# A two-layer transformer trunk on one core: the residual update that closes a feed-forward split moves into the next split's first block

## What is computed

```
h = rms_norm(x) * (1.0 + sc2) + sh2
x = x + g2 * swiglu(h, ffn_w_in[layer], ffn_w_out[layer])
# swiglu: gate, up = split(h @ w_in, 2);  (silu(gate) * up) @ w_out
```

## Time and profile before

| what | value |
| --- | --- |
| median of three runs | 2400.76 us |
| lowest and highest run | 2396.38, 2400.95 us |
| span of the profiled execution (its own time) | 2402.0 us |
| TensorE (PE) busy | 2210.0 us, 92% |
| VectorE (DVE) busy | 1744.0 us, 73% |
| ScalarE (ACT) busy | 955.6 us, 40% |
| mean granted TensorE clock | 0.982 of full speed |
| mean DMA rate | 247 GB/s |

### The profile page before, as it was taken

The page is one execution under the profiler, slowest core; times in us unless marked ns, Lnnn a source line. Parts: engine busy times, 40 slices in busy tenths (PEclk is TensorE's granted clock), DMA queues, the critical chain, the costliest instruction groups (busy, mean ns, idle before and its releaser), DMA issues.

```text
span 2402.0 us, 27802 instructions
## 1 busy us (share of the span) xinstructions
PE 2210.0 (92%) x10348; PEld 1841.0 (77%) x10348; DVE 1744.0 (73%) x2089; ACT 955.6 (40%) x1236; POOL 10.1 (0%) x23
## 2 busy tenths in 40 slices
PE   0199999989999999999998999898999999999997
PEld 0178888778888788887886788787888788887886
DVE  6898889898779877898777856498775545554454
ACT  1054444435443344433444344244443344433443
POOL 0000000000000000000000000000000000000000
PEclk9999999999999999999999999899999999999999
DMA  8876776786768877788766632285774455554533
GB/s 334 348 302 271 286 278 245 296 333 250 277 264 330 342 281 287 267 357 314 286 244 250 236 122 99 97 330 220 281 280 174 177 178 190 192 193 175 189 150 151
DMA packets 82438, 593.12 MB, mean 247 GB/s; under 512 B 9409, under 2 KB 9441, under 8 KB 10785
## 3 DMA queue, kind: packets, MB, share of 16 engines
q1 hardware_dynamic: 81056, 587.25, 63.8%
q0 software_dynamic: 1280, 4.51, 0.7%
HBM read 589.62 MB, written 2.10 MB: 246 GB/s over the span
## 4 chain that ended last, share of the span: by engine, by line
PE 43%; issue 36%; DVE 13%; DMA 4%; DVEq 2%; ACT 2%; SPq 0%; POOL 0%; ACTq 0%; POOLq 0%
PE ps L1164 12%; PE ps L1166 12%; PE ps L1165 12%; DVE acc L699 6%; DMA ada_raw<-in_ada 4%; DVE w_lo L677 3%; PE ps L1153 2%; DVE work L970 1%; DVE x L973 1%; DVEq L971 1%; PE ps L1231 1%; PE ps L1236 1%; PE ps L1234 1%; PE ps L1250 0%; PE ps L1248 0%
## 5 line engine op out<-in xcount | busy, mean ns | idle before, releaser
L431 ACT ACTIVATE w_hi<-raw 128x1024 fp32r<-128x1024 f32 x728 | 767.9, 1061 | 1087.8 <-PE ps L1166 989.2
L677 DVE TENSOR_TENSOR w_lo<-raw,w_hi 128x1024 fp32r<-128x1024 f32 x728 | 887.9, 1222 | 427.5 <-ACT w_hi L431 424.4
L1164 PE MATMUL ps<-w_hi,xT_hi 128*128 128x512 f32 x1952 | 773.8, 396 | 31.3 <-DVE w_lo L677 22.5
L1166 PE MATMUL ps<-w_hi,xT_lo 128*128 128x512 f32 x1952 | 765.4, 392 | 0.0
L1165 PE MATMUL ps<-w_lo,xT_hi 128*128 128x512 f32 x1952 | 764.8, 392 | 0.0
L699 DVE SCALAR_TENSOR_TENSOR acc<-ada_raw,cond,acc 128x512 f32<-128x512 f32 (+1 forms) x656 | 485.8, 747 | 19.6 <-DMA ada_raw<-in_ada 12.4
L1164 PEld LDWEIGHTS ps<-w_hi,xT_hi 128*128 128x128 f32 x1952 | 369.7, 189 | 110.4 <-issue 31.9
L1166 PEld LDWEIGHTS ps<-w_hi,xT_lo 128*128 128x128 f32 x1952 | 369.3, 189 | 78.5
L1165 PEld LDWEIGHTS ps<-w_lo,xT_hi 128*128 128x128 f32 x1952 | 369.8, 189 | 74.7
L1164 PE MATMUL ps<-w_hi,hT_hi 128*128 128x512 f32 x960 | 377.3, 393 | 5.0 <-DVE w_lo L677 2.9
L1166 PE MATMUL ps<-w_hi,hT_lo 128*128 128x512 f32 x960 | 374.3, 390 | 0.0
(11 more groups left out here) (145 smaller groups left out, 931.9 us busy)
## 6 DMA issues: line engine op xcount, KB each, us to landing
ada_raw<-in_ada SPq DMA_DIRECT2D x176, 1024.0 KB, 6.6
raw<-in_ffn_in SPq DMA_DIRECT2D x176, 1024.0 KB, 4.8
raw<-in_ffn_out SPq DMA_DIRECT2D x88, 1024.0 KB, 6.3
raw<-in_ab_in SPq DMA_DIRECT2D x48, 1024.0 KB, 7.2
raw<-in_swa_in SPq DMA_DIRECT2D x20, 1024.0 KB, 5.4
raw<-in_ada SPq DMA_DIRECT2D x16, 1024.0 KB, 10.6
raw<-in_ab_out SPq DMA_DIRECT2D x16, 1024.0 KB, 7.0
raw<-in_swa_out SPq DMA_DIRECT2D x16, 1024.0 KB, 7.2
```

The costliest lines, as they stand in the source:

```text
L431: nc.scalar.activation(w_hi[:, p % PAIRS, :, :], raw[:, t % RAW, 2 * (p % 2):2 * (p % 2) + 2, :], ACT.Copy).then_inc(hi_ready, 1)
L677: tt(w_lo[:, p % PAIRS, :, :], raw[:, (p // 2) % RAW, 2 * (p % 2):2 * (p % 2) + 2, :], w_hi[:, p % PAIRS, :, :].bitcast(F32), ALU.subtract ...
L1164: mm(out, hi[:, kt, tok], w_hi[:, q % PAIRS, k, :], start=(kt == 0), stop=False)
L1166: last = mm(out, lo[:, kt, tok], w_hi[:, q % PAIRS, k, :], start=False, stop=(kt == 2 * ph.pairs - 1))
```

## The change

VectorE no longer issues the update of output block 3 behind the output stage of splits 0 and 1. It issues it in the first iteration of the next split's input stage, behind the `lo` of pair 3 (and ahead of that pair's ada step). The semaphore value that it waits for is the same count, written from the new stage's side. No other engine's code is touched.

```
@@ -1024,6 +1024,8 @@
                                     gated(fin, h0, 2 * i + b - 1, 1 - b)
                                 if p == 5 and not (first and b == 0):
                                     hidden_lo(h0, 2 * i + b - 1, 1 - b)
+                                if first and s and n == 3:
+                                    update(NB - 1, 1, USED_CREDIT + 2 * fin.quad0)
                                 if first and summed_in and n in (8, 15):
                                     columns(summed_in, n // 15)
                                 ada_behind(fin, i, n)
@@ -1051,8 +1053,6 @@
                     repeat(dve, 1, fin.n, body)
                     out_body(0, True)
                     repeat(dve, 1, fout.n, out_body)
-                    if s < 2:
-                        update(NB - 1, 1, used(NB - 1))
                     h0 += 2 * fin.n
```

## The result

| | before | changed |
| --- | --- | --- |
| median of the timed runs | 2398.82 us | 2374.51 us |
| lowest and highest | 2396.38, 2400.95 | 2372.14, 2375.92 |
| span of the profiled execution | 2402.0 us | 2370.2 us |
| TensorE's waits for a `lo` | 25.4 us in 13 | 9.0 us in 7 |

The ratio is 0.9900, with a 95% interval of 0.9886 to 0.9914: 24.3 us faster. The forecast was 2375.8 us, 25.0 us faster. A fourth run of before came with the result, hence the new median of 2398.82.

What follows compares the result with a forecast made beforehand. The prediction took the kernel to be bound by matmuls, with losses at four seams. Gains of 12.5 us in each layer made 25.0 us, so 2375.8 us against 2400.76, with a range of 2371 to 2382.

Steps and rivals of the forecast that it cites:

- The gap's cause: At each seam between stages, pair 0's `lo` stood behind the update in VectorE's queue; first TensorE wait 3.84 us.
- The size: Loss at the four seams: 25.6 us in sum, some 16 of idling and 9.6 of slow matmuls.
- ruler: Time between ScalarE's conversions of pairs 3 and 7 across a seam, less the undisturbed 10.88 us for four pairs.
- The ada delay in layer 0: First seam: a late ada quad holds the step ahead of pair 1's `lo`, costing TensorE 0.5 to 0.6 us.
- The narrowest place: First seam, layer 0: `lo` of pair 4 done at 828.7, wanted at 829.1, a margin of 0.4 us.
- Layer 1's lead: After the old stage's last matmul, pair 4's `lo` ends at 6.2 us; TensorE wants it at 10.9 us.
- The loads moved relative to the matmuls: SyncE's quad 4 loads, issued up to 4 us later, might delay the second ada quad; taken as nothing, up to 1 us.
- The sum: Gains of 12.5 us in layer 1 and 12.5 us in layer 0, together 25.0 us.
- The slower rival: At the seams TensorE's first new block waits for the moved update after all: 11 us slower, 2412; chance 0.03.

Runs made afterwards that it cites:

- the filled gap: Kernel before, with 17 unread matmuls put on TensorE at the head of each split's first block at the seams: 2388.39 us against 2397.91, ratio 0.9956.
- layer 0 alone: Update moved only at the two seams of layer 0, layer 1 as in the kernel before: 2388.56 us, ratio 0.9958 to before.

## Why the prediction was right, step by step

**The gap's cause** (the `lo` of pair 0 stood behind the update): shown. With the update behind `lo` 3 TensorE doesn't stop at pair 0; behind `lo` 0 it stops at pair 1 for as long as the queue says; a wait on TensorE's side alone brings the gap back.

**The size.** The ruler's 25.6 us are the very loss in the trace of before, since all four seams read zero after. Its split in 16 and 9.6 is shown by the filled gap (16.3 and 9.3). The times agree within their intervals, 24.3 and 27.3 us. That the fourth seam lost less belongs to the execution and not to the seam: in the trace with layer 0 alone the third lost 5.67 us and the fourth 6.82, the other way round than in before.

**The ada delay in layer 0, 0.6 us:** right in kind, wrong for the execution profiled. The quad landed 8.4 us after its issue, as the 8.5 of the earlier trace rows, but it was issued at 807.52, 7.9 us ahead of T, and not 7.0. How early it is issued goes with how far VectorE is ahead of TensorE. In the six traces with the step in its old place the `lo` of pair 0 started 2.80, 2.81, 2.21, 1.95, 1.95 and 1.57 us before T, and the step behind it, held by the quad, started at T + 0.62, 0.56, 1.20, 1.34, 1.47 and 1.80. Pair 1 follows the step's start by 1.67 us and is wanted at T + 2.72, so it came 0, 0, 0.15, 0.30, 0.43 and 0.75 us late. The prediction's 0.6 came from the trace of before, where VectorE was free for this `lo` 1.87 us before T (815.80). So it was a term of most executions, though not of the one profiled with the result, and its size runs from nothing to 0.75.

**The narrowest place,** `lo` of pair 4 in the first seam: ended at 825.45, wanted at 815.38 + 10.88 = 826.26, a lead of 0.8 where I had 0.4. **Layer 1's lead** of 4.7 us is shown from both sides: 3.9 us more fit in, 7.8 overdraw it by 3.07.

**The loads moved relative to the matmuls:** no TensorE gap from them in the changed kernel. Quad 4 was issued at 817.65, T + 2.3. That is 5.0 us behind the second ada quad (812.69), where in before the distance was 7.3 us (815.83 and 823.08). The ada quad landed 10.7 us after its issue, at 823.4, where before it took 10.8. So quad 4, in flight beside it for 5.7 us in place of 3.5, held it up by nothing that can be seen; the delay of a microsecond or two that equal shares would have made did not come. That is one load in two traces, and what loads in flight do to each other was not tried otherwise.

**The sum,** 25.0 us, was taken from an execution that the prediction put 1.2 us above the median. A span reads about 2 us less than the time of the same execution (2370.2 against 2372.14 for the changed kernel), so it was rather 3 us above it. The forecast doesn't depend on this, since it takes 25.0 off the median. The whole change measured 24.3 and 27.3 us in two sets of runs, so the forecast is within what the runs can tell.

**The slower rival** had 11 us over before, measured 10.3, by the gaps that it named: 8.42 + 7.91 + 5.05 + 5.04 less 4 x 4.00 is 10.4. By the ruler it is 37.7 less 25.6, 12.1. It did not come true because the credit of `evacuated` is two.

## What to carry to other kernels

In an in-order queue, an instruction that waits for another engine's last act holds up everything behind it that was ready; put it behind as much ready work as that engine will consume before it needs the result, and count the chain from the latest arrival in it (here the ada quad), not from the event waited for. Price a stall of TensorE with the slow matmuls behind it: here 4.0 us of gap cost 5.6 to 6.8. When two profiles differ by more than the medians do, cut both at the same instructions before crediting the change.

## What the hardware showed that I had not expected

The same gap of 4.00 us cost 5.62 to 6.82 us over eight seams in three traces, so the slow matmuls behind it cost 1.6 to 2.8, and at one and the same seam now more, now less; the price of one seam is not known to better than a microsecond. Behind a gap of 3.07 us the granted clock was 0.54 and 0.52 over the next 3.2 us, as behind that of 4.00 (0.50 to 0.52), while behind gaps of 1.59 us and less it was 1.00; between them nothing was tried. And executions of one code differed by up to 3.9 us on the way to the first seam and by up to 3.6 us between the second and third (6.5 with the traces whose loss there was taken off), which is more than the seam losses themselves vary; what causes it wasn't looked into.
